# Sparse attention's units by block of four heads, with the first output slab's turns and products placed between the later units

## The reference, cut to what matters

```python
q, k, v, qi, ki, wi = split(u @ c_w_in)          # rope on q, k, qi, ki
score = einsum(relu(qi @ ki), wi) + causal
sel = top_k(score, 64)
s = q @ k[sel] * 128 ** -0.5                      # 16 heads, 4 of them to a key/value head
o = softmax(s) @ v[sel]                           # (256, 2048)
m = o @ c_w_out                                   # 2048 x 2048
h = h + rms_norm(m, g)
```

## Time and profile before

| | |
|---|---|
| median of 3 runs | 2527.29 us (2526.68 to 2529.71) |
| the profiled execution | 2527.35 us, with a span of 2525.6 us |
| TensorE busy | 2475.8 us, 98% |
| VectorE busy | 1442.4 us, 57% |
| ScalarE busy | 1109.8 us, 44% |
| mean granted TensorE clock | 0.996 |

### The profile page before, as it was taken

One profiled execution on the slowest core, in us unless ns is written; L12 is line 12 of the kernel. 1 busy time (PEld: TensorE's weight loads), 2 busy tenths in 40 slices (PEclk: granted clock), 3 DMA queues, 4 the chain that ended last, 5 costly groups with the idle time before them and its releaser, 6 DMA issues.

```text
span 2525.6 us, 31818 instructions
## 1 busy us (share of the span) xinstructions
PE 2475.8 (98%) x13495; PEld 2056.0 (81%) x13495; DVE 1442.4 (57%) x1565; ACT 1109.8 (44%) x1240; POOL 151.1 (6%) x173
## 2 busy tenths in 40 slices
PE   8999999999999999999998999999999999999998
PEld 6888778788888888888887977788888888888886
DVE  5557775665545545445566667556544545545565
ACT  5445532464334334334455445555434334334453
POOL 4000324100000000000100000000000000000000
PEclk9999999999999999999999999999999999999999
DMA  8556511645555555565554655355556555555554
GB/s 257 189 177 212 187 31 70 221 167 191 192 188 192 187 190 188 188 196 190 189 192 134 205 165 165 138 183 174 187 189 195 187 188 191 189 190 193 192 187 147
DMA packets 225138, 454.26 MB, mean 180 GB/s; under 512 B 7897, under 2 KB 16407, under 8 KB 223723
## 3 DMA queue, kind: packets, MB, share of 16 engines
q1 hardware_dynamic: 219165, 430.63, 51.6%
q0 software_dynamic: 3936, 18.59, 2.2%
q10 hardware_dynamic: 1902, 3.07, 0.4%
HBM read 446.57 MB, written 2.10 MB: 178 GB/s over the span
## 4 chain that ended last, share of the span: by engine, by line
PE 92%; DVE 5%; ACT 2%; issue 1%; DMA 1%; DVEq 0%; SPq 0%; ACTq 0%
PE psum L307 28%; PE psum L309 28%; PE psum L308 28%; DVE wlo L296 1%; PE psum L805 1%; PE psum L1827 1%; PE psum L1818 1%; PE psum L421 1%; DMA raw<-in_ab_w_in 0%; PE psum L1144 0%; PE psum L1145 0%; PE psum L1146 0%; ACT whi L291 0%; PE psum L1807 0%; DVE h L627 0%
## 5 line engine op out<-in xcount | busy, mean ns | idle before, releaser
L296 DVE TENSOR_TENSOR wlo<-raw,whi 128x2048 fp32r<-128x2048 f32 (+1 forms) x408 | 936.1, 2301 | 706.6 <-ACT whi L291 706.0
L291 ACT ACTIVATE whi<-raw 128x2048 fp32r<-128x2048 f32 (+1 forms) x408 | 774.4, 1904 | 756.1 <-DMA raw<-in_w_mlp_down 327.3
L307 PE MATMUL psum<-whi,uTh 128*128 128x512 f32 (+2 forms) x2176 | 851.0, 391 | 9.3 <-DVE uTl L443 3.9
L309 PE MATMUL psum<-whi,uTl 128*128 128x512 f32 (+2 forms) x2176 | 842.2, 387 | 0.0
L308 PE MATMUL psum<-wlo,uTh 128*128 128x512 f32 (+2 forms) x2176 | 841.7, 387 | 0.0
L307 PEld LDWEIGHTS psum<-whi,uTh 128*128 128x128 f32 x2176 | 409.4, 188 | 96.8 <-issue 10.6
L309 PEld LDWEIGHTS psum<-whi,uTl 128*128 128x128 f32 x2176 | 409.3, 188 | 81.7
L308 PEld LDWEIGHTS psum<-wlo,uTh 128*128 128x128 f32 x2176 | 409.6, 188 | 78.4 <-issue 0.5
L307 PE MATMUL psum<-whi,hTh 128*128 128x512 f32 x1024 | 399.9, 390 | 0.0
L309 PE MATMUL psum<-whi,hTl 128*128 128x512 f32 x1024 | 398.6, 389 | 0.0
L308 PE MATMUL psum<-wlo,hTh 128*128 128x512 f32 x1024 | 398.4, 389 | 0.0
(11 more groups left out here) (373 smaller groups left out, 1467.7 us busy)
## 6 DMA issues: line engine op xcount, KB each, us to landing
raw<-in_w_mlp_up SPq DMA_DIRECT2D x128, 1024.0 KB, 5.4
raw<-in_w_mlp_down SPq DMA_DIRECT2D x128, 1024.0 KB, 5.0
raw<-in_ab_w_in SPq DMA_DIRECT2D x48, 1024.0 KB, 5.2
raw<-in_w_ple_gate SPq DMA_DIRECT2D x32, 1024.0 KB, 5.0
raw<-in_c_w_in SPq DMA_DIRECT2D x24, 1024.0 KB, 5.3
raw<-in_ab_w_out SPq DMA_DIRECT2D x16, 1024.0 KB, 5.6
raw<-in_c_w_out SPq DMA_DIRECT2D x16, 1024.0 KB, 5.1
raw<-in_c_w_in SPq DMA_DIRECT2D x12, 736.0 KB, 4.5
```

Source lines behind the costliest of these rows:

```text
L291: act.activation(whi[:, q, :, 0:n], raw[:, q, :, 0:n], ACT.Copy).then_inc(hi_ready, 1)
L296: dve.tensor_tensor(wlo[:, q, :, 0:n], raw[:, q, :, 0:n], whi[:, q, :, 0:n].bitcast(F32), ALU.subtract).then_inc(lo_ready, 1)
L307: pe.matmul(o, xh, hi, start=(q == 0 and k == 0), stop=False)
L309: last = pe.matmul(o, xl, hi, start=False, stop=(q == 3 and k == 3))
```

## The change

1. The units go by block of four heads (`a_units`): for each block b the pairs 2b and 2b+1 of tile 0, then the same of tile 1.
2. PSUM: both heads' scores of a unit share a bank (6 or 7), turned weights stay in 4 or 5, the products with the values have bank 2 alone, the turned result has bank 3 (its last two groups 4 and 5). The first output slab has banks 0 and 1.
3. Scores, mask, maximum and exponential of units 0 and 1 move ahead of the end of c_in: the scores before the last queries' turn, the mask behind the last step of the selection, the exponential ahead of the values slab's eviction.
4. Six of the eight groups of turns go into the loop of the units (behind units' iterations 8, 10, ... 18), and seven of the sixteen k-blocks of slab 0 (`c_out_blocks`) behind iterations 12 to 18. ACT's and DVE's parts of groups 0 to 4 come one iteration later, and the splits of chunks 2 and 3 in iterations 11 and 15 (ACT), 12 and 16 (DVE). Each group's high and low part is one instruction over 512 columns.
5. The separate start of c_out is left out for this stage.

```diff
+    a_units = [(tt, 2 * b + p_) for b in range(4) for tt in range(TT) for p_ in range(2)]
+    SC_BANK, PT_BANK, PV_BANK, ZT_BANK = (6, 7), (4, 5), 2, (3, 3, 3, 3, 3, 3, 4, 5)
...
             if t == t_tr:
+                if n == 4:
+                    pe.wait_ge(sem("qc_out"), 2 * n)
+                    c_scores_pe(pe, 0)
+                    c_scores_pe(pe, 1)
...
+                if tt == 1:
+                    c_mask_dve(dve, 0)
+                    c_mask_dve(dve, 1)
...
+            if i == N_C - 1:
+                c_exp_act(act, 0)
+                c_exp_act(act, 1)
             act.wait_ge(mm_used, 4 * (b + i) + 4)
...
+    def c_values_pe(pe, u):
+
+        tt, hp, nk = unit(u)
+        pe.wait_ge(sem("c_wT"), u + 1)
+        if u >= 1:
+            pe.wait_ge(sem("c_y"), u)
...
+    def c_turn_pe(pe, g):
+
+        st = "c_out"
+        pe.wait_ge(sem("c_y"), 4 * (g // 2) + 4)
+        if 0 < g < 6:
+            pe.wait_ge(*mark("xT_lo", st, g))
+        if g == 6:
+            pe.wait_ge(sem("c_wT"), nu)
...
+    def c_turn_low(dve, g):
+
+        st = "c_out"
+        dve.wait_ge(*mark("xT_hi", st, g + 1))
...
+    def c_out_blocks(pe, q, blocks):
+
+        st, s = "c_out", base["c_out"]
+        if q == 0 and blocks[0] == 0:
+            pe.wait_ge(*free_of(st, 0))
+        if blocks[0] == 0:
+            pe.wait_ge(lo_ready, 4 * s + q + 1)
+            pe.wait_ge(*mark("xT_lo", st, 2 * q + 2))
+        last = mm_chunk(pe, q, s % 2, W, range(TT), (uTh, uTl), blocks)
...
+    TURNS = {8: 0, 10: 1, 12: 2, 14: 3, 16: 4, 18: 5}
...
+        for i in range(2, nu + 3):
             if i < nu:
...
+                c_scores_pe(pe, i)
+            if i == 2:
+                c_weights_pe(pe, 0)
+                pe.wait_ge(sem("ev_c_in"), N_C)
+            if 1 <= i - 2 < nu:
+                c_weights_pe(pe, i - 2)
+            if 0 <= i - 3 < nu:
+                c_values_pe(pe, i - 3)
+            if i in TURNS:
+                c_turn_pe(pe, TURNS[i])
+            if i >= 12 and i - 12 < 7:
+                c_out_blocks(pe, (i - 12) // 4, range((i - 12) % 4, (i - 12) % 4 + 1))
+        c_out_blocks(pe, 1, range(3, 4))
+        c_out_blocks(pe, 2, range(0, 2))
+        c_turn_pe(pe, 6)
+        c_turn_pe(pe, 7)
+        c_out_blocks(pe, 2, range(2, 4))
+        c_out_blocks(pe, 3, range(4))
...
+        for i in range(2, nu + 3):
+            if i < nu:
+                c_exp_act(act, i)
             if 0 <= i - 3 < nu:
...
                 last.then_inc(sem("c_y"), 1)
+            if i - 1 in TURNS:
+                c_turn_high(act, TURNS[i - 1])
+            if i in (11, 15):
+                split_hi(act, s, {11: 2, 15: 3}[i])
...
             if i < nu:
...
+                c_mask_dve(dve, i)
+            elif i - 2 < nu:
+                c_copy_dve(dve, i - 2)
+                c_recip_dve(dve, i - 2)
+            if i - 1 in TURNS:
+                c_turn_low(dve, TURNS[i - 1])
+            if i in (12, 16):
+                split_lo(dve, s, {12: 2, 16: 3}[i])
```

More of the change, by code:

```diff
@@ L297, in split_lo, with mm_chunk @@
                           ALU.subtract).then_inc(lo_ready, 1)
-    def mm_chunk(pe, q, par_, n, tiles, lhs):
-        for k in range(4):
+    def mm_chunk(pe, q, par_, n, tiles, lhs, blocks=range(4)):
+        for k in blocks:
             for tt in tiles:
@@ L2469, in c_pool, with unit, c_scores_pe @@
             pool.dma_start(ikg[:, i, :], A[n][0].partition_broadcast(P)).then_inc(sem("ikg_in"), 16)
+    def unit(u):
+        tt, hp = a_units[u]
+        return tt, hp, (tt + 1) * P
+    def c_scores_pe(pe, u):
+        tt, hp, nk = unit(u)
+        if u >= 2:
+            pe.wait_ge(sem("c_masked"), u - 1)
+        for j in range(2):
+            last = pe.matmul(bank[SC_BANK[u % 2]][:, j * nk:(j + 1) * nk], qTc[:, 2 * hp + j, tt * P:(tt + 1) * P],
+                             kTc[:, hp // 2, 0:nk], start=True, stop=True)
+        last.then_inc(sem("c_scores"), 1)
@@ new lines, in c_weights_pe @@
+    def c_weights_pe(pe, u):
+        tt, hp, nk = unit(u)
+        pe.wait_ge(sem("c_exp"), 2 * u + 2)
+        if u >= 2:
+            pe.wait_ge(sem("c_wT"), u - 1)
+        for j in range(2):
+            for kb in range(tt + 1):
+                q = j * (tt + 1) + kb
+                last = pe.transpose(bank[PT_BANK[u % 2]][:, q * P:(q + 1) * P], pc[:, u % 2, j, kb * P:(kb + 1) * P],
+                                    ident[:])
+        last.then_inc(sem("c_tr"), 1)
+    def c_values_pe(pe, u):
+        tt, hp, nk = unit(u)
+        pe.wait_ge(sem("c_wT"), u + 1)
+        if u >= 1:
+            pe.wait_ge(sem("c_y"), u)
+        for j in range(2):
+            c = j * P
+            for kb in range(tt + 1):
+                last = pe.matmul(bank[PV_BANK][:, c:c + P], pcT[:, u % 2, j * (tt + 1) + kb, :],
+                                 zc[:, kb, C2 + (hp // 2) * P:C2 + (hp // 2 + 1) * P],
+                                 start=(kb == 0), stop=(kb == tt))
+        last.then_inc(sem("c_pv"), 1)
@@ new lines, in c_turn_pe @@
+    def c_turn_pe(pe, g):
[5 more added lines that the diff above has]
+            pe.wait_ge(sem("c_wT"), nu)
+        for kk in range(2):
+            for tt in range(TT):
+                c = (2 * g + kk) * P
+                last = pe.transpose(bank[ZT_BANK[g]][:, (2 * kk + tt) * P:(2 * kk + tt + 1) * P], zc[:, tt, c:c + P],
+                                    ident[:])
+        last.then_inc(sem("xT"), 1)
@@ L2472, in c_pe @@
+    def c_out_blocks(pe, q, blocks):
[6 more added lines that the diff above has]
+        last = mm_chunk(pe, q, s % 2, W, range(TT), (uTh, uTl), blocks)
+        if blocks[-1] == 3:
+            last.then_inc(mm_used, 1)
+    TURNS = {8: 0, 10: 1, 12: 2, 14: 3, 16: 4, 18: 5}
     def c_pe(pe):
@@ new lines, in c_pe, with c_exp_act @@
+        c_out_blocks(pe, 2, range(0, 2))
[3 more added lines that the diff above has]
+        c_out_blocks(pe, 3, range(4))
+    def c_exp_act(act, i):
+        tt, hp, nk = unit(i)
+        act.wait_ge(sem("c_max"), i + 1)
+        if i >= 2:
+            act.wait_ge(sem("c_tr"), i - 1)
+        for j in range(2):
+            act.activation(pc[:, i % 2, j, 0:nk], smc[:, i % 2, j, 0:nk], ACT.Exp, bias=mxc[:, i % 2, 2 + j:3 + j],
+                           accum_out=mxc[:, i % 2, 4 + j:5 + j]).then_inc(sem("c_exp"), 1)
@@ L2498, in c_pe, with c_act @@
+    def c_act(act):
+        s = base["c_out"]
+        for i in range(2, nu + 3):
+            if i < nu:
+                c_exp_act(act, i)
             if 0 <= i - 3 < nu:
                 u = i - 3
[L2500 to L2526, removed]
+                tt, hp, nk = unit(u)
@@ new lines, in c_act, with c_mask_dve @@
+            if i in (11, 15):
+                split_hi(act, s, {11: 2, 15: 3}[i])
+        for g in (5, 6, 7):
+            c_turn_high(act, g)
+    def c_mask_dve(dve, i):
+        tt, hp, nk = unit(i)
+        dve.wait_ge(sem("c_scores"), i + 1)
+        if i >= 2:
+            dve.wait_ge(sem("c_exp"), 2 * (i - 1))
+        x = bank[SC_BANK[i % 2]][:, 0:2 * nk].rearrange("p (c k) -> p c k", c=2)
+        y = smc[:, i % 2, :, 0:nk]
+        dve.scalar_tensor_tensor(out=y, in0=x, scalar=C_HD ** -0.5,
+                                 in1=mb[:, tt, 0:nk].unsqueeze(1).broadcast_to([P, 2, nk]), op0=ALU.mult,
+                                 op1=ALU.add).then_inc(sem("c_masked"), 1)
+        if i >= 2:
+            c_copy_dve(dve, i - 2)
+        dve.wait_ge(sem("c_masked"), i + 1)
+        dve.tensor_reduce(mxc[:, i % 2, 0:2], y, AX.X, ALU.max).then_inc(sem("c_top"), 1)
+        if i >= 2:
+            c_recip_dve(dve, i - 2)
+        dve.wait_ge(sem("c_top"), i + 1)
+        if i >= 2:
+            dve.wait_ge(sem("c_rl"), i - 1)
+        dve.tensor_scalar(mxc[:, i % 2, 2:4], mxc[:, i % 2, 0:2], -1.0, None, ALU.mult).then_inc(sem("c_max"), 1)
@@ new lines, in c_copy_dve, with c_recip_dve @@
+    def c_copy_dve(dve, u):
+        nq = 2 * (a_units[u][0] + 1)
+        dve.wait_ge(sem("c_tr"), u + 1)
+        if u >= 2:
+            dve.wait_ge(sem("c_pv"), u - 1)
+        dve.tensor_copy(pcT[:, u % 2, 0:nq, :], bank[PT_BANK[u % 2]][:, 0:nq * P]).then_inc(sem("c_wT"), 1)
+    def c_recip_dve(dve, u):
+        dve.wait_ge(sem("c_exp"), 2 * u + 2)
+        if u >= 4:
+            dve.wait_ge(sem("c_y"), u - 3)
+        dve.reciprocal(rlc[:, u % 4, :], mxc[:, u % 2, 4:6]).then_inc(sem("c_rl"), 1)
@@ L2535, in c_dve @@
     def c_dve(dve, link):
-        for i in range(nu + 2):
+        s = base["c_out"]
+        for i in range(2, nu + 3):
             if i < nu:
[L2538 to L2570, removed]
```

51 lines of the change are left out of this document (16 added, 35 removed).

## The result

The changed kernel takes 2534.28 us (median of 14 runs, 2530.45 to 2535.98), the kernel before 2527.93 us (14 runs). The ratio is 1.0024, with a 95% interval of 1.0017 to 1.0032: 6.1 us slower, with 4.3 to 8.1 as bounds. The profiled execution has a span of 2530.4 us, 4.8 above that of before. Its page says at once that TensorE's work is the same: it is as busy as before, on a longer span.

A forecast was written before the change was run, and what follows sets the result against it. TensorE, busy 98% of the span, was taken as the bound. The walk put slab 1 at 1636.1 against 1630.1, +5.9 us on 2527.35, so 2533.3 us, 0.2% slower; range 2527.5 to 2537.5.

The forecast's parts named there:

- the ring: Units' loop, once in two units: values, scores, mask to exponential, exponential, result, next values; 6.03 us tile 1, 4.16 tile 0.
- the stretch: TensorE from c_in's last matmul to slab 1's first, 62.4 us before; all that the change was said to touch.
- Part 1: Units 0 and 1 start before c_in ends: some 2.5 us gained; ACT 1.0 us late, TensorE waits 0.4 at the eviction.
- Part 2: One bank for the values makes the ring bind: 10.19 us in four units, 2.55 a unit against 1.8 before.
- The walk: Unit-by-unit pass through three engines' orders with profiled durations: slab 1 at 1636.1, against 1630.1 for the kernel before.
- Part 3: Turns and blocks between units: DVE waits 2.1 to 2.4 us at five groups; seven blocks fill part of TensorE's waits.
- The sum: Slab 1 at 1636.1 against 1630.1 gives +5.9 us on 2527.35: 2533.3 us, 0.2% slower.
- Everything behind slab 1 only shifts: After slab 1's first matmul no time is lost; POOL's later loads cost nothing, as nothing needs them before slab 2.
- the ring doesn't bind: Rival, units' loop: one more bank may not matter; slab 1 at 1631.6, +1.5, total 2528.8 us; chance 0.17.
- Filled waits: Rival, loop with blocks: TensorE fills its waits, a pair of units under 5 us; 2517 to 2522 us; chance 0.11.
- 51.7 + 0.5: TensorE's own work from c_in to slab 1, 51.7 us, plus 0.5 for switches: where filled waits would lead.
- The clock: Rival: TensorE's clock falls behind idle, 1.6 us for one fall; two or three give 2536 to 2538; chance 0.14.

The follow-up runs named there:

- result_first: The changed kernel with ACT making a unit's result before it waits for the next exponential, still one bank for the values: 2526.61 us, ratio 1.0001.
- both_first: The changed kernel with ACT's order in each iteration turned to high part, result, exponential: 2521.32 us, ratio 0.9982.
- one_bank_before: The kernel before with the values in one bank, each unit's values waiting for the previous unit's result, nothing else changed: 2538.98 us, ratio 1.0054.
- high_first: The changed kernel with ACT's high part of each turned group 0 to 4 ahead of the exponential in the same iteration: 2532.68 us, ratio 1.0024.
- block_order: The kernel before with only the units' order changed to the new one (two of tile 0, two of tile 1): 2529.87 us, ratio 1.0009.
- units_alone_two: The changed kernel without turns and blocks in the units' loop and with two banks for the values: 2532.49 us, ratio 1.0017.
- early_units: The kernel before with only scores, masks and exponentials of units 0 and 1 moved ahead of c_in's end: 2524.22 us, ratio 0.9987.

## Why the prediction was right

The forecast was +5.9 us (2533.3); measured were +6.1 by the ratio and 2534.28 in the median, inside the range and on the side with the highest chance. The mechanism held, the ring above all. That the number came within 0.2 us is luck: the forecast put all of it into the stretch, which lost 4.6 us and not 5.9, and nothing behind it, where 1.5 us were lost.

*Part 1.* Unit 2's mask starts 1.94 us after c_in, scores included, where it was 4.43 (1572.55 - 1568.12): 2.5 us, as forecast, and TensorE's wait for the values' eviction is 0.28 and not 0.4. ACT wasn't the 1.0 us late that the forecast had: its exponentials were done when c_in's last matmul was (1567.88), and the eviction began 0.04 us later. The run with part 1 alone gives 2.8 us in the stretch.

*Part 2, the ring.* This was the step that decided, and it held in its size. The walk's times lie 1.3 us late against the trace up to unit 7 (values of unit 1 at 1575.7 and 1574.42, of unit 7 at 1591.0 and 1589.68), because c_in ended 1.28 us sooner in this execution; between them it is exact to 0.1. Forecast 10.19 us in four units: from the values of unit 1 to those of unit 5 the trace has 10.30 (1574.42 to 1584.72); in the kernel before with one bank 6.04 for two units of tile 1. Its single waits are smaller than forecast (1 to 2 us in most units): ten units wait, and four of them 0.99 to 1.84 us, the others 0.19 to 0.83. By result_first 5.8 of the 10.6 us that both_first takes off the changed kernel go with the ring alone; the turns' waits give the rest only once the ring is open.

*Part 3.* Forecast were DVE's waits of 2.1 to 2.4 us at five groups; they are 1.94 and 2.15 at four, and 0.60 at the fifth, whose turn comes when no exponential is left. The forecast counted five. The end of the walk is a little long: from the values of unit 9 (1596.30) to those of unit 15 (1617.98) are 21.7 us where it had 22.3. That, 0.2 us behind the units and 0.1 ahead of unit 9 make the stretch 67.0 and not 68.0. TensorE's idle time in it is 11.1 us (66.13 - 55.04), where the walk had 14. The seven blocks and the two turns behind the loop came as said, with TensorE without idle from 1620 to slab 1.

*The sum.* The stretch is thus 1.0 us shorter than forecast, and the walk of the kernel before was 0.45 too short: +4.6, not +5.9. On the other side stands "Everything behind slab 1 only shifts", which was wrong. The forecast saw POOL's loads move closer to slab 1 and said that nothing needs them before slab 2; it left out that they share the DMA engines with slab 1's own loads, which is the reading above for the wait. TensorE waited 1.13 us in slab 1, and all in all 1.5 were lost there. The two errors, 1.3 and 1.5 us, nearly cancel.

*The rivals.* That the ring doesn't bind is refuted by one_bank_before and result_first. Filled waits: from the values of unit 9 to those of 11 there are 8.0 us, so no. But the bound that I named, a pair of units with blocks under 5 us, was wrong: TensorE's own work in such a pair is 3.3 of units, 2.7 of blocks and 0.5 of a turn, and both_first, which has 6.9 us there (1587.75 to 1594.60), is faster than the kernel before. And the argument against it, that ACT can't be ahead since it waits for each unit's maximum, was only true of the order in the diff: with result and high part first, ACT has its work done in that very wait, and the stretch comes to 56.4 us, 4.2 above the 51.7 + 0.5 of the bound. The clock: it did not fall in the changed kernel, with 1.84 us as its longest wait in the loop; but it did in four of the others (high_first, one_bank_before, block_order, units_alone_two), so that it was not a far-fetched case.

*The bank rule and the transposes.* The rule of the Trainium skill, "PSUM — Partial Sum Buffer", section "PSUM bank collisions raise a hardware error", that two engines must not be on one bank together, was priced at the difference between one bank and two, 4.5 us. Result_first keeps the rule, one bank and the wait on the unit before, and still ends 5.8 us lower: the rule forces the wait, not its length. No run here shows a collision. The Trainium skill, "TensorE: Matmul & The Clock Gate", section "Part 4: PE-mode transpose", says that transposes don't count as busy the same way as matmuls. In high_first the stretch ahead of the first fall has transposes and scores mixed, and the same stretch in the changed kernel doesn't fall. No run here separates the share of the transposes.

## What to carry to other kernels

When a buffer goes from two to one, don't ask how long its user needs it, but what stands ahead of its release on the releasing engine: here a 0.6 us result stood behind an exponential that waited for a third engine, and a step of one engine became a ring through three. An engine that waits for one thing should have done before it all that is ready; moving 0.6 us of work from behind a wait to ahead of it gave 5.8 us, nearly twice as much as the earlier start. And to fill TensorE's gaps late in a loop, count first what the filling takes from buffers and from the other engines' orders in all the iterations before it. Last, follow every wait on the last step of the moved work: here loads for a later stage came 2.5 us nearer to the next slab, and 1.2 to 1.8 us were lost there in every kernel that had it.

## What the runs showed of the hardware that was not expected

The granted clock falls to half behind waits that are short. In high_first it does behind 0.44 and 1.84 us of idle with 0.66 of transposes between, in the same place in three profiles of three; in the changed kernel the same waits (0.44 and 1.84), at the same distance from c_in's end, pass without a fall in three of three. The 1.83 us ahead of slab 0 are likewise in four kernels, with a fall about 1.5 us behind them in block_order and one_bank_before and none in the kernel before and early_units (one profile each). One fall cost 1.3 us in the units and 1.6 in a stream of 512-column matmuls (eight, 0.43 apart). What tells high_first and the changed kernel apart, whose instructions up to there are in the same order, is open.
